# Two dense blocks in one program: a different start of the first expert unit, bounded gathers, a reordered queue, and another schedule for the last output tiles

## The reference, cut to what matters

```python
h = modulate(x, sh2, sc2)
x = x + g2[:, None, :] * hier_moe(h, w_group, b_group, w_router, b_router, w13, w2)
x = rms_norm(x) * final_norm_w                       # end of the first block
h = rms_norm_2(x, norm_mix)
x = x + sliding_window_sink_attention(h, swa_w_in, sinks, swa_w_out)
x = x + swiglu_ffn(rms_norm_2(x, norm_ffn), ffn_w_gate_up, ffn_w_down)
return rms_norm_2(x, final_norm)
```

## Time and profile before

| what | us |
|---|---|
| median of 3 executions | 2122.27 (2121.68 to 2122.73) |
| the profiled execution | 2120.99 |
| its span, first to last instruction | 2119.2 |
| PE, VectorE, ScalarE, GpSimd busy | 1963.4, 1404.3, 1012.7, 702.9 |

### The profile page before, as it was taken

The page is one execution under the profiler, slowest core; times in us unless marked ns, Lnnn a source line. Parts: engine busy times, 40 slices in busy tenths (PEclk is TensorE's granted clock), DMA queues, the critical chain, the costliest instruction groups (busy, mean ns, idle before and its releaser), DMA issues. The chain is left out here.

```text
span 2119.2 us, 45175 instructions
## 1 busy us (share of the span) xinstructions
PE 1963.4 (93%) x15296; PEld 1473.5 (70%) x15296; DVE 1404.3 (66%) x2178; ACT 1012.7 (48%) x1463; POOL 702.9 (33%) x479
## 2 busy tenths in 40 slices
PE   5899998899798999988879989999999999999998
PEld 4788877688454555544457866687788888878787
DVE  7888628733597999978755359657755555475564
ACT  5211228412597999967732039434333333343333
POOL 1333311131010111011045636333554444545553
PEclk9999999999899999999989989999999999999999
DMA  7644114346899999999953200121332333264233
GB/s 284 248 151 148 40 61 160 123 176 261 330 419 422 390 380 421 422 422 422 421 195 100 90 25 1 70 70 50 120 97 91 109 104 104 75 242 174 65 134 124
DMA packets 100910, 410.07 MB, mean 194 GB/s; under 512 B 10492, under 2 KB 21596, under 8 KB 75484
## 3 DMA queue, kind: packets, MB, share of 16 engines
q1 hardware_dynamic: 81820, 366.79, 45.5%
q10 hardware_dynamic: 13680, 22.81, 2.9%
q0 software_dynamic: 5328, 19.40, 2.5%
HBM read 357.53 MB, written 51.43 MB: 193 GB/s over the span
## 5 line engine op out<-in xcount | busy, mean ns | idle before, releaser
L1832 PE MATMUL moe_hu<-places,acc_sq 128*32 128x256 f32 x5120 | 309.0, 388 | 25.4 <-DVE places L1700 12.5
L1700 DVE COPY places<-places 128x2048 f32 (+1 forms) x240 | 242.5, 1043 | 59.2 <-DMA places<-in_w 26.6
L1832 PEld LDWEIGHTS moe_hu<-places,acc_sq 128*32 128x32 f32 x5120 | 162.7, 112 | 151.8 <-DVE places L1700 26.1
L1700 ACT ACTIVATE places<-places 128x2048 f32 (+1 forms) x159 | 235.6, 1482 | 57.5 <-PE moe_hu L1832 31.3
L2738 PE MATMUL ff_bank<-xh,ff_u_hi 128*128 128x512 f32 x480 | 189.7, 395 | 9.9 <-DVE x_late L3218 6.6
L2699 POOL TENSOR_TENSOR ff_u_lo<-ff_sums,ff_u_hi 128x512 fp32r<-128x512 f32 x120 | 165.5, 1390 | 93.9 <-ACT ff_u_hi L2865 93.9
L2699 POOL TENSOR_TENSOR ff_u_lo<-ff_raw,ff_u_hi 128x512 fp32r<-128x512 f32 x90 | 124.2, 1380 | 216.2 <-ACT ff_u_hi L2865 216.2
L2738 PE MATMUL ff_bank<-xh,ff_u_lo 128*128 128x512 f32 x480 | 188.5, 393 | 0.0
L2738 PE MATMUL ff_bank<-xl,ff_u_hi 128*128 128x512 f32 x480 | 188.5, 393 | 0.0
L1843 PE MATMUL moe_y<-places,moe_at 128*32 128x256 f32 x2560 | 153.5, 380 | 8.1 <-DVE moe_at L1922 5.0
L1791 POOL COPY moew_idx<-rows 128x1 int32 (+1 forms) x20 | 18.2, 909 | 414.3 <-PE moe_xturn L1819 414.3
(11 more groups left out here) (517 smaller groups left out, 4532.7 us busy)
## 6 DMA issues: line engine op xcount, KB each, us to landing
places<-in_w SPq DMA_DIRECT2D x192, 1024.0 KB, 16.1
ff_raw<-in_w_up SPq DMA_DIRECT2D x44, 512.0 KB, 3.6
blk_scratch<-x_late SPq DMA_DIRECT2D x56, 256.0 KB, 4.1
w_early<-in_w_qkv SPq DMA_DIRECT2D x24, 512.0 KB, 3.5
in_w_raw<-in_w_in SPq DMA_DIRECT2D x23, 512.0 KB, 3.6
xbc<-in_w_ada SPq DMA_DIRECT2D x20, 512.0 KB, 8.1
y_scratch<-moe_ysb ACTq DMA_DIRECT2D x78, 128.0 KB, 7.4
ff_raw<-in_w_down SPq DMA_DIRECT2D x16, 512.0 KB, 3.5
```

The costliest lines, as they stand in the source:

```text
L1700: m = e.activation(to, src, ACT.Copy) if k == "act" else e.tensor_copy(to, src)
L1832: m = e.matmul(hu[u % 2][rows(j), 0:2 * FW].rearrange("p (a f) -> p a f", a=2), xt[:, t, rows(u)], w[:, :, FW * j:FW * (j + 1)], start=(t ...
```

## The change

- The 12 dummy products before group 0 are taken out, and the six in the route stage become five.
- SP loads `x_late` and sends its two results first, and then loads `w_early`.
- In the middle stage ScalarE casts the high part of the two early weight tiles, ahead of its scalings; VectorE only subtracts.
- In the tail the eight turned tiles go to banks 0, 1, 0, 1, 0, 3, 1, 2. Tiles 0 to 3 are turned behind j = 2, 4, 5 and 6 of the second half. Behind the last tile PE turns seven of the eight blocks of tiles 4 and 5, then adds the token sums, then turns seven blocks of tile 6, then the last block of the three, then tile 7. ScalarE evicts tiles 4 and 6, VectorE 5 and 7. Every tile has a buffer of its own, except that tile 3 takes tile 0's, after that was stored; tiles 4 to 7 go where the first half's x was.

The diff, without the lines around it:

```diff
@@ -54,6 +54,7 @@
+NO_TOKEN = float(T)
@@ -73,7 +74,7 @@
-               ("prio", NE), ("rank_at", NE)):
+               ("prio", NE), ("rank_at", NE), ("tokless", NT)):
@@ -1431,7 +1432,7 @@
-                                         in_offset=bass.IndirectOffsetOnAxis(ap=self.idx[:, 0:1], axis=0)).then_inc(self.s_g, 16)
+                                         in_offset=bass.IndirectOffsetOnAxis(ap=self.idx[:, 0:1], axis=0), bounds_check=T - 1, oob_is_err=False).then_inc(self.s_g, 16)
@@ -1477,7 +1478,7 @@
-                    self.warm(e, turned[0], 6)
+                    self.warm(e, turned[0], 5)
@@ -1613,7 +1614,7 @@
-                        do(e.tensor_tensor(one_g_r[:, c, :], one_g[:, c, :], over(self.const("tokid").unsqueeze(2), NT, NB), ALU.mult))
+                        do(e.tensor_tensor(one_g_r[:, c, :], one_g[:, c, :], over(self.const("tokless").unsqueeze(2), NT, NB), ALU.mult))
@@ -1627,7 +1628,7 @@
-                    do(e.tensor_copy(self.rows[:, :], small[:, NT:NT + NB]), "rows")
+                    do(e.tensor_scalar(self.rows[:, :], small[:, NT:NT + NB], NO_TOKEN, None, ALU.add), "rows")
@@ -1774,14 +1775,14 @@
-                    left(last - RING + (W_PLACE - self.place(0, last)) % RING)
-                    for b in range(2):
-                        e.dma_start(self.w_early[:, b, :], self.ins["w_qkv"][b]).then_inc(self.s_wqkv[b], 16)
                     for k in range(KT // 2):
                         left(last - RING + (X_PLACE + k - self.place(0, last)) % RING)
                         e.dma_start(self.x_late[:, 2 * k:2 * k + 2, :], self.xt_dram[:, 2 * k:2 * k + 2, :]).then_inc(self.s_spill, 16)
                     for j in range(CT // 2):
                         send(e, n, j)
+                    left(last - RING + (W_PLACE - self.place(0, last)) % RING)
+                    for b in range(2):
+                        e.dma_start(self.w_early[:, b, :], self.ins["w_qkv"][b]).then_inc(self.s_wqkv[b], 16)
@@ -1792,7 +1793,7 @@
-                                             in_offset=bass.IndirectOffsetOnAxis(ap=idx[:, 0:1], axis=0)).then_inc(s_g, 16)
+                                             in_offset=bass.IndirectOffsetOnAxis(ap=idx[:, 0:1], axis=0), bounds_check=T - 1, oob_is_err=False).then_inc(s_g, 16)
@@ -1850,7 +1851,6 @@
-                    self.warm(e, hu[0], 12)
@@ -2135,6 +2135,9 @@
+                    for b in range(2):
+                        e.wait_ge(g.s_loaded[b], 16)
+                        e.activation(g.hi[:, b, :], g.raw[:, b, :], ACT.Copy).then_inc(g.s_first, 1)
@@ -2162,7 +2165,10 @@
-                    g.first(by=e)
+                    e.sem_inc(g.s_split, 2)
+                    for b in range(2):
+                        e.wait_ge(g.s_first, b + 1)
+                        e.tensor_tensor(g.lo[:, b, :], g.raw[:, b, :], g.hi[:, b, :].bitcast(F32), ALU.subtract).then_inc(g.s_split, 1)
@@ -2531,7 +2537,10 @@
-            otok = [rstd[:, :], sums[:, 2:4, :].rearrange("p s c -> p (s c)")]
+            otok = [rstd[:, :].rearrange("p (s c) -> p s c", s=2), sums[:, 2:4, :], sums[:, 0:2, :], rstd[:, :].rearrange("p (s c) -> p s c", s=2)]
+            otok += [x[:, k:k + 2, A] for k in range(0, KT, 2)]
+            turned_in = [bank[0], bank[1], bank[0], bank[1], bank[0], bank[3], bank[1], bank[2]]
+            AFTER_TURN = {2: 0, 4: 1, 5: 2, 6: 3}
@@ -2541,7 +2550,7 @@
-            s_o = [st.sem(f"o{b}") for b in range(2)]
+            s_out0, s_out = st.sem("out0"), st.sem("out")
@@ -2680,10 +2689,11 @@
-                        st.wait(e, st.act, f"otok{t}")
-                        e.dma_start(self.out[t * P:(t + 1) * P, :], otok[t % 2]).then_inc(s_o[t % 2], 16)
-                    for b in range(2):
-                        e.wait_ge(s_o[b], 16 * HT)
+                        st.wait(e, st.dve if t in (HT + 1, HT + 3) else st.act, f"otok{t}")
+                        rows = self.out[t * P:(t + 1) * P, :].rearrange("p (s c) -> p s c", s=2)
+                        e.dma_start(rows, otok[t]).then_inc(s_out if t else s_out0, 16)
+                    e.wait_ge(s_out0, 16)
+                    e.wait_ge(s_out, 16 * (NT - 1))
@@ -2828,24 +2838,33 @@
-                    def turn(t):
+                    def turn(t, first, end):
...
-                        st.wait(e, st.act, f"z{h}{KT - 1}")
-                        if t >= 2:
-                            st.wait(e, st.act, f"otok{t - 2}")
-                        for k in range(KT):
-                            m = e.transpose(bank[t % 2][:, k * P:(k + 1) * P], x[:, k, at:at + P], self.const("ident"))
-                        st.pe(m, f"turned{t}")
+                        st.wait(e, st.act, f"z{h}{end - 1}")
+                        for k in range(first, end):
+                            m = e.transpose(turned_in[t][:, k * P:(k + 1) * P], x[:, k, at:at + P], self.const("ident"))
+                        if end == KT:
+                            st.pe(m, f"turned{t}")
...
-                        elif h == 1 and j % 2 == 0:
-                            turn(j // 2 - 1)
-                    turn(HT - 1)
+                        elif h == 1 and j in AFTER_TURN:
+                            t = AFTER_TURN[j]
+                            if t >= 2:
+                                st.wait(e, st.act, f"otok{t - 2}")
+                            turn(t, 0, KT)
+                    st.wait(e, st.act, "otok2")
+                    turn(HT, 0, KT - 1)
+                    e.wait_ge(gd.s_emptied, 2 * KT + 2)
+                    turn(HT + 1, 0, KT - 1)
...
-                    for t in range(HT, NT):
-                        turn(t)
+                    st.wait(e, st.act, "otok3")
+                    turn(HT + 2, 0, KT - 1)
+                    for t in range(HT, HT + 3):
+                        turn(t, KT - 1, KT)
+                    st.wait(e, st.dve, "inv1")
+                    turn(HT + 3, 0, KT)
@@ -3007,9 +3026,9 @@
-                        if t >= 2:
-                            e.wait_ge(s_o[t % 2], 16 * (t // 2))
-                        st.act(e.activation(otok[t % 2], bank[t % 2][:, :], ACT.Copy, scale=rt[:, t:t + 1]), f"otok{t}")
+                        if t == 3:
+                            e.wait_ge(s_out0, 16)
+                        st.act(e.activation(otok[t], turned_in[t][:, :].rearrange("p (s c) -> p s c", s=2), ACT.Copy, scale=rt[:, t:t + 1]), f"otok{t}")
@@ -3017,6 +3036,8 @@
+                        if h and j - 1 in AFTER_TURN:
+                            out(AFTER_TURN[j - 1])
@@ -3025,12 +3046,9 @@
-                        elif h == 1 and j % 2 == 1:
-                            out(j // 2 - 1)
-                    out(HT - 1)
...
-                    for t in range(HT, NT):
-                        out(t)
+                    out(HT)
+                    out(HT + 2)
@@ -3277,6 +3295,10 @@
+                    st.wait(e, st.act, "rt1")
+                    for t in (HT + 1, HT + 3):
+                        st.wait(e, st.pe, f"turned{t}")
+                        st.dve(e.tensor_scalar(otok[t], turned_in[t][:, :].rearrange("p (s c) -> p s c", s=2), rt[:, t:t + 1], None, ALU.mult), f"otok{t}")
@@ -3334,6 +3356,7 @@
+    consts[:, CONSTS["tokless"]] = k[:, None] + P * np.arange(NT) - NO_TOKEN
...
```

## The result

The changed kernel took 2109.37 us (median of 4 runs, 2105.59 to 2111.24), the kernel before 2122.5 (4 runs, 2121.68 to 2125.8): a ratio of 0.9933, 95% interval 0.9916 to 0.9950. Run once more beside other kernels (6 runs) it took 2107.93, ratio 0.9937 (0.9925 to 0.9949). The profiled execution took 2111.24 us (span 2109.4), the longest of its four; a second profile of the same kernel has a span of 2103.9.

A forecast was written before the change was run, and what follows sets the result against it. The DMA stream was taken to set the time for most of the expert stage. Terms 6.6 + 4.1 + 3.5 + 0.3 + 1.8 = 16.3 us off the profiled 2120.99 gave 2104.7, or 2106.0 as median; range 2100 to 2113.

The forecast's parts named there:

- Part 1: First expert unit: without the dummies the first reload moves 9.1 us earlier and DMA's gap closes, 6.6 us, bounds 3 to 7.
- the hole: Stretch over 561 to 573 us, around the first expert unit, where DMA runs dry (share 0.46); sized at 6.6 us.
- rival (b): First expert units: reloads are late behind a cold PE and half the DMA gap stays, 2109.3 us; chance 0.12.
- Rival (e): Expert stage: without the dummies the clock stays low, each unit costing 5.5 us more; 2144 if low until 650; chance 0.06.
- Part 2: Expert gathers: empty slots, 20% of all, are no longer moved, saving 4.1 us, bounds 0 to 5.
- Rival (a): Gathers: rows out of bounds are still moved, so 4.1 us and 1.2 at the stage's end go, 2111.3; chance 0.15.
- the two between meet the hole at 740: Expert stage: two gather savings fall where PE is the bound and DMA half idle, so 0.3 us comes off 4.4.
- Part 3: Border from experts to middle stage: two result stores no longer queue behind 1 MB of attention weights, 3.5 us, bounds 1 to 5.
- Part 4: Middle stage's start: two weight casts move from DVE to ACT, covered by the gather wait, 0.3 us, bounds -4.6 to 0.7.
- Rival (d): Middle stage's start: the attention weights land late, 4.6 us worse, 2110.6; chance 0.05.
- Part 5: Last tiles: reordered turns, evictions and stores end the span 13.5 instead of 15.3 us after the old product end, saving 1.8.
- Rival (c): Stores at the middle stage's border and the end interfere less than charged, 2.0 and 1.5 us more gained, 2102.5; chance 0.12.

The follow-up runs named there:

- the warm start: Changed kernel with 18 calls (36 records) of dummy products behind the route stage's last product: 2108.7 us, ratio 0.9936 to the kernel before.
- the start alone: Kernel before with only the 12 dummy products ahead of group 0 taken out and the route stage's six made five: 2115.9 us, ratio 0.9963.
- 12 late dummies: Changed kernel with 12 dummy products behind the route stage's last product: 2108.57 us, ratio 0.9930 to the kernel before.
- bound, order and tail: Kernel before with one edit each: empty slots out of the gathers' bounds (0.9984), weight loads behind x loads and result stores (0.9989), whole new tail (0.9989).
- the bound undone: Changed kernel with its gathers as before (index 0 for an empty slot, no bounds check): 2110.27 us, ratio 0.9950 to the kernel before.

## Why the prediction was nearly right

**Part 1, 6.6 forecast; 7.6 to 8.1 measured.** Mechanism, place and sign were right: the reload moved by 10.0 (9.1 forecast), the hole closed (rival (b) is out), PE's cold units took 1.1 to 1.5 us of its lead, and the warm start showed that these would have been worth nothing. The term was mis-sized by the column I read. I took the hole from the share, 12 x (1 - 0.46/1.02) = 6.6. The same row has 156 GB/s against 422, and 12 x (1 - 156/422) is 7.6. The share overstates the work done there (0.46 of the time for 0.37 of the rate); a stage that is bound by a stream is paid in bytes. A good part of it is the second gather, over 564 to 572 of the kernel before:

```profile
q0 software_dynamic: 144, 0.52, 21.8%
```

It kept the engines busy for 21.8% of 8 us, 1.74 us, where a gather in the full stream takes 1.2 to 1.3. The route's sixth dummy gave 0 instead of 0.6: the product ended 0.5 us earlier after the route's start (27.9 against 28.4), but the first gather was issued at 29.6 to 29.7 with and without the edit (the start alone, and the kernel before), for DVE reached its cast of `rows` no sooner.

By the Trainium skill, "TensorE: Matmul & The Clock Gate", section "What's actually happening", "the default state is throttled, and activity releases the throttle". The kernel with 12 late dummies shows both halves (1.00, then 0.53 after 4.46 us of idle time). Rival (e) took that rule to its end; in fact the clock was at 0.50 under the first products only until 562, at 0.57 over 562 to 564, and at 1.00 from 564 to 916. The dips behind that (0.66 over 916 to 926) stand in the kernel before as well (0.62 over 926 to 936).

**Part 2, 4.1 forecast; 2.4 measured among the experts.** Rival (a) is out: exactly 640 rows were not moved. The term itself was a little too small: the 8.91 MB are 17 gathers, not 18, which makes 430 x 0.051 / 17 = 1.29 us each and 0.26 for a fifth. The step that failed is "the two between meet the hole at 740", for which I took off 0.3 us. The hole is no spot of ten microseconds but the visible part of a stretch of 160 us, from 710 to 870, that PE sets. In the table the bound gains nothing within it. How the missing 1.7 us divide is open: the two gathers ahead of the idle time are 0.5, another 0.7 was missing at the stretch's start already, and behind it less came than the gathers there could give. I had the row that points to it (PE 9.78 of 10, DMA 0.51 at 740 to 750) and did not ask how far PE's bound reaches.

**Part 3, 3.5 forecast; 2.5 measured, by either of two edits.** Over the profiles with neither edit the border is 6.7 us on average (7.83, 6.23, 6.15), with both 4.25. The first of these is the only one that I had. And I added the order's 2.5 to the empty last gather's 1.2; they are one gain. The kernel with the 12 dummies back fits that: with them the other edits together gave only 4.5 us (ratio 0.9979), against 8.1 by the sum of the single ratios of bound, order and tail. The border's double count is 2.5 of these 3.6, and the rest is within the intervals.

**Part 4, 0.3 forecast; about 0.2 measured.** From the table load to the first scaling: 7.28 on average in the nine profiles with the split (7.12 to 7.46), 7.51 in the five without (7.37 to 7.63). The weights landed after 3.9 us (under 6 forecast); ACT's two casts took 1.06 each and lay under the gather. Rival (d) is out. The split wasn't run alone, so that it is the cause of the 0.2 is not shown.

**Part 5, 1.8 forecast; 1.3 to 1.5 measured.** The new tail takes 13.1 us from DVE's last add, not 12.6. The window at 2103 to 2108 has 382 GB/s where I took 400 from two stores: 5.5 us for 2 MB, not 5.2; and the first byte moved 1.3 us after the first issue and the last landing came 0.5 after the last byte, while I had charged 1.3 once. Against these 0.8 stands a first issue 0.2 us sooner (5.4 after the add, 5.6 forecast). The Trainium skill's formula ("DMA: Bandwidth & Descriptors", "Anatomy of one DMA"), with its estimated 1.5, came nearer. That may be luck: the page gives it as a fit for GpSimd's DMA path, these stores are SP's, and its 3.2 us for one of them is too long, for the stores with nothing beside them landed in 2.6 here. Rival (c) is out.

**The sum.** 7.9 + 2.4 + 2.5 + 0.2 + 1.3 = 14.3 us, against 13.1 and 14.6 measured, with about 1 us of doubt in the first two terms. One term was too small by 1.3 and four too large by 3.3 in all; that 2106.0 came within 3.4 us of the time is in part luck, for these went against each other.

## What to carry to other kernels

When two resources set a stage's pace in turn, find the length of every stretch that each one sets before you add up savings. A saving counts if it moves the one that sets the pace at that place: the closed hole did, for PE's progress stood 8 us sooner from then on, while PE's own microsecond from the warm start was gone five gathers later, and the lighter gathers gained nothing over the 160 us that PE sets. The markers of progress (here the gathers) of several kernels, laid side by side from a common start, show it. Price a hole of a stream in bytes, not in busy share. Two edits that empty the same queue in front of the same wait are one term.

## What the runs showed beyond that

- A gather with indices out of bounds keeps its packets (2592 over 600 to 1030 with the bound and with the bound undone) and moves only the rows within: 7.36 MB against 9.44.
- DMA issues on SP grew from 0.33 us for a store of a whole tile that runs alone to 0.61 to 1.28 for each of the last four, which follow one another; taking one of them to another queue saved nothing.
- PE's first work of the expert stage (a dummy before, the turn after) starts 10.8 and 10.0 us behind the issue of the first gather in the profiles before and after, and 10.3 with 24 records of dummy products in this gap, which cost nothing; with 36 records, which ended at 555.94, it is 11.0. That the stage's border waits for that gather's landing fits, but wasn't tried.
